# Layer norm weight and bias applied on ScalarE after the transpose, operand sums moved to VectorE, and other places for the turns

## What is computed

```
def _post(x, mix, ln1_g, ln1_b, w_up, w_down, ln2_g, ln2_b):
    h = _layernorm(DEEPNORM_ALPHA * x + mix, ln1_g, ln1_b)      # mix = concat(...) @ w_out
    f = square(relu(h @ w_up)) @ w_down
    return _layernorm(DEEPNORM_ALPHA * h + f, ln2_g, ln2_b)
```

## Time and profile before

| | us |
|---|---|
| median of 3 runs | 1950.86 (1946.68 to 1951.31) |
| profiled execution | 1942.62 |
| its span | 1940.8 |
| PE busy / DVE / ACT / POOL | 1752.3 / 1164.2 / 676.3 / 538.6 |
| mean granted TensorE clock | 0.948 |

### The profile page before, as it was taken

How to read it: one execution, slowest core, us unless ns; L and a number is a source line. 1 busy time by engine, 2 the same in 40 slices (tenths; PEclk the granted TensorE clock), 3 DMA queues, 4 the chain that set the end, 5 groups by cost and what they waited for, 6 DMA issues and landing times. The chain is left out here.

```text
span 1940.8 us, 41181 instructions
## 1 busy us (share of the span) xinstructions
PE 1752.3 (90%) x16969; PEld 1490.3 (77%) x16969; DVE 1164.2 (60%) x2079; ACT 676.3 (35%) x1467; POOL 538.6 (28%) x413
## 2 busy tenths in 40 slices
PE   6999996898899989988797996999999899989995
PEld 5999993676666666666576875999999888768884
DVE  7611025557776675665343898666666465565887
ACT  2221212344544544544232133322322244444441
POOL 0000003322232222222100455555565330322510
PEclk9999996898999999998698997999999999999997
DMA  5552230110111011010516231444444487555553
GB/s 189 187 192 95 73 95 20 49 49 14 70 63 61 2 61 62 2 61 13 149 24 240 91 116 44 131 138 144 150 126 125 146 287 237 166 176 164 194 183 121
DMA packets 155079, 218.86 MB, mean 113 GB/s; under 512 B 32290, under 2 KB 94394, under 8 KB 153876
## 3 DMA queue, kind: packets, MB, share of 16 engines
q1 hardware_dynamic: 153572, 211.53, 33.1%
q0 software_dynamic: 1328, 4.78, 0.6%
HBM read 151.66 MB, written 65.43 MB: 112 GB/s over the span
## 5 line engine op out<-in xcount | busy, mean ns | idle before, releaser
L1513 PE MATMUL c_p<-c_d_b_hi,c_d_a_hi 128*128 128x512 f32 x448 | 177.9, 397 | 14.2 <-DVE c_d_b_lo L1306 13.8
L1513 PE MATMUL c_p<-c_d_b_lo,c_d_a_hi 128*128 128x512 f32 x448 | 176.2, 393 | 0.0
L1513 PE MATMUL c_p<-c_d_b_hi,c_d_a_lo 128*128 128x512 f32 x448 | 175.9, 393 | 0.0
L1300 DVE TENSOR_TENSOR c_d_a_lo<-c_a_raw,c_d_a_hi 128x512 fp32r<-128x512 f32 x112 | 92.3, 824 | 62.4 <-ACT c_d_a_hi L1087 62.0
L1477 PE MATMUL c_p<-c_T_hi,c_up_op_hi 128*128 128x288 f32 x512 | 111.6, 300 | 12.7 <-DVE c_T_lo L1210 10.3
L1087 ACT ACTIVATE c_d_a_hi<-c_a_raw 128x512 fp32r<-128x512 f32 x112 | 70.2, 627 | 137.3 <-PE c_p L1513 128.2
L1513 PEld LDWEIGHTS c_p<-c_d_b_hi,c_d_a_hi 128*128 128x128 f32 x448 | 85.3, 190 | 37.1 <-issue 14.7
L1477 PE MATMUL c_p<-c_T_lo,c_up_op_hi 128*128 128x288 f32 x512 | 111.4, 300 | 0.0
L1477 PE MATMUL c_p<-c_T_hi,c_up_op_lo 128*128 128x288 f32 x512 | 111.3, 299 | 0.0
L1206 DVE TENSOR_TENSOR c_up_op_lo<-c_up_raw,c_up_op_hi 128x512 fp32r<-128x512 f32 x80 | 93.6, 1175 | 26.8 <-ACT c_up_op_hi L1022 26.8
L307 ACT ACTIVATE a_o<-a_pO 128x308 f32<-128x308 f32 (+1 forms) x80 | 32.7, 408 | 217.7 <-PE a_pO L446 200.9
(11 more groups left out here) (495 smaller groups left out, 4477.3 us busy)
## 6 DMA issues: line engine op xcount, KB each, us to landing
c_a_raw<-scratch_ops SPq DMA_DIRECT2D x112, 256.0 KB, 2.8
c_d_r<-w_down SPq DMA_DIRECT2D x96, 256.0 KB, 3.2
c_up_raw<-w_up SPq DMA_DIRECT2D x32, 512.0 KB, 5.2
scratch_ops<-c_hid SPq DMA_DIRECT2D x64, 256.0 KB, 2.5
scratch_ops<-c_h_sum SPq DMA_DIRECT2D x48, 256.0 KB, 2.0
scratch_p<-a_o SPq DMA_DIRECT2D x72, 154.0 KB, 1.8
m_pr<-w_in SPq DMA_DIRECT2D x8, 1232.0 KB, 7.8
m_pr<-scratch_p SPq DMA_DIRECT2D x8, 1232.0 KB, 5.3
```

What stands on the lines that cost most here:

```text
L1300: dve.tensor_tensor(lo[:, :], a_raw[a % 4][:, :], hi[:, :].bitcast(F32), ALU.subtract).then_inc(S("da_lo"), 1)
L1513: last = pe.matmul(bank, d_a[a % DA_RING][x][:, P * p:P * p + P], d_b[b % DB_RING][w][:, :], start=m in (1, 2, 5) and j == 0 and n == 0, s ...
```

## The change

- POOL's `h1` and DVE's `h1_last` go: all nine tiles end with DVE's normalise, are stored and turned without weight and bias. The store and the turn wait for `h1_normed`.
- ACT applies weight and bias in the turned layout, where they are one number per partition: `h1_copies` has one instruction per 128 columns with a scale and a bias pointer (columns of `ln1_g`, `ln1_b`, loaded as 128x8). The high parts for half 0 are then copied from SBUF.
- As the stored h1 lacks weight and bias, `prepare` on POOL applies them to the y tiles before `begin`: five tiles in round m = 1 behind the steps in `PREPARE_AT`, four behind the last step of round m = 6. The rows of `ln1_g` and `ln1_b` (512 KB each) are loaded behind step 4 of round m = 1 instead of in the output projection.
- `differences` and the T4 subtraction move from POOL to DVE; `w_sums(0)` also waits for the last `h1_normed`.
- `scales` for one column uses 9 small steps instead of 12.
- The turns move inside the out products, and turn 7 moves in; DVE's, ACT's and SP's orders follow. Products 4 and 5 are issued in halves.

In the diff the indentation is shortened.

```diff
@@ -491,6 +491,7 @@
+PREPARE_AT = (6, 8, 10, 12, 14)
@@ -501,8 +502,9 @@
 DA_RING, DB_RING, DR_RING = 4, 9, 8
-TURN_AT = {(3, 3): ("mix", 4), (4, 3): ("mix", 5), (4, 7): ("h1", 0), (5, 3): ("mix", 6), (5, 7): ("h1", 1), (6, 1): ("h1", 2),
-           (6, 3): ("mix", 7), (6, 5): ("h1", 3), (6, 7): ("h1", 4), (7, 3): ("mix", 8), (7, 7): ("h1", 5), (8, 3): ("h1", 6)}
+TURN_AT = {(3, 3): ("mix", 4), (4, 3): ("mix", 5), (4, 5): ("h1", 0), (4, 7): ("h1", 1), (5, 1): ("h1", 2), (5, 3): ("mix", 6),
+           (5, 6): ("h1", 3), (6, 1): ("h1", 4), (6, 3): ("mix", 7), (6, 6): ("h1", 5), (7, 3): ("mix", 8), (7, 6): ("h1", 6),
+           (8, 6): ("h1", 7)}
...
@@ -731,10 +734,7 @@
+    sp.wait_ge(S("h1_normed"), i + 1)
@@ -770,30 +770,31 @@
+    sp.dma_start(columns[n][:, :], io[n].rearrange("(k p) -> p k", p=P), allow_slow_non_contiguous=True).then_inc(S(f"{n}_landed"), 16)
 load_h(3)
...
@@ -878,6 +879,9 @@
         load_step(i, j)
+        if m == 1 and j == 4:
+            for n in ("ln1_g", "ln1_b"):
+                sp.dma_start(rows1[n][:, :], bcast(io[n])).then_inc(S(f"{n}_landed"), 16)
         if m == 1 and j == 5:
@@ -897,26 +901,16 @@
 -def h1(i):
-    if i == 0:
-        pool.wait_ge(S("ln1_g_landed"), 16)
-        pool.wait_ge(S("ln1_b_landed"), 16)
-    pool.wait_ge(S("h1_normed"), i + 1)
-    x = of(i)[:, :]
-    pool.tensor_tensor(x, x, rows1["ln1_g"][:, :], ALU.mult).then_inc(S("h1_scaled"), 1)
-    pool.wait_ge(S("h1_scaled"), i + 1)
-    pool.tensor_tensor(x, x, rows1["ln1_b"][:, :], ALU.add).then_inc(S("h1_ready"), 1)
...
+def prepare(n, T):
+    if n == 0:
+        pool.wait_ge(S("ln1_g_landed"), 32)
+        pool.wait_ge(S("ln1_b_landed"), 32)
+    pool.wait_ge(S(f"y_landed{T}"), 16)
+    x = y[T][:, :]
+    pool.tensor_tensor(x, x, rows1["ln1_g"][:, :], ALU.mult).then_inc(S("y_scaled"), 1)
+    pool.wait_ge(S("y_scaled"), n + 1)
+    pool.tensor_tensor(x, x, rows1["ln1_b"][:, :], ALU.add).then_inc(S("y_prepared"), 1)
@@ -924,6 +918,7 @@
         pool.wait_ge(S("out_summed"), N_TILE)
+        pool.wait_ge(S("h1_normed"), N_TILE)
     else:
@@ -951,14 +946,7 @@
-for i in range(7):
-    h1(i)
-for i in range(4, 8):
-    differences(i)
 w_sums(0)
-differences(8)
-pool.wait_ge(S("T2_summed"), 2)
-pool.tensor_tensor(HT["21"][:, :, :], HT["21"][:, :, :], HT["22"][:, :, :], ALU.subtract).then_inc(S("T4_summed"), 1)
 w_sums(1)
@@ -971,11 +959,16 @@
                 .then_inc(S("t_summed"), 1)
+            if j in PREPARE_AT:
+                prepare(PREPARE_AT.index(j), (SAMPLE_TILE, 0, 1, 2, 3)[PREPARE_AT.index(j)])
         if m == 6:
...
                 .then_inc(S("t_summed"), 1)
+            if j == NJ - 1:
+                for T in range(4, 8):
+                    prepare(T + 1, T)
         if m in (7, 4):
@@ -1002,12 +995,21 @@
+        if i == 0 and u == 0:
+            act.wait_ge(S("ln1_g_landed"), 16)
+            act.wait_ge(S("ln1_b_landed"), 16)
+        for k in range(KH):
+            c = slice(KH * u + k, KH * u + k + 1)
+            for half, src, cols in places(i):
+                last = act.activation(HT[quarter(u, half)][:, k, cols], bank[:, k, src], ACT.Identity,
+                                      scale=columns["ln1_g"][:, c], bias=columns["ln1_b"][:, c])
+        last.then_inc(S("h1_copied"), 1)
+    for u in range(2):
         for half, src, cols in places(i):
             if half == 0:
-                act.activation((B11, B21)[u][0][:, :, cols], bank[:, :, src], ACT.Copy).then_inc(S("side_hi"), 1)
-        for half, src, cols in places(i):
-            last = act.activation(HT[quarter(u, half)][:, :, cols], bank[:, :, src], ACT.Copy)
-        last.then_inc(S("h1_copied"), 1)
+                act.wait_ge(S("h1_copied"), copy_no["h1", i, u])
+                act.activation((B11, B21)[u][0][:, :, cols], HT[quarter(u, 0)][:, :, cols], ACT.Copy)\
+                   .then_inc(S("side_hi"), 1)
@@ -1048,28 +1050,27 @@
         h1_copies(t)
-    if (kind, t) == ("h1", 5):
+    if (kind, t) == ("h1", 6):
         act.wait_ge(S("out_summed"), 7)
         for q in range(3):
             up_high(q)
-act.wait_ge(S("out_summed"), 8)
-up_high(3)
-h1_copies(7)
+        act.wait_ge(S("out_summed"), 8)
+        up_high(3)
 act.wait_ge(S("out_summed"), N_TILE)
 act.wait_ge(S("h1_copied"), copy_no["h1", 7, 1])
 high(B22, HT["22"], EARLY_COLS, "B22_hi")
+h1_copies(8)
 act.wait_ge(S("T1_summed"), 4)
 high(T1, HT["11"], EARLY_COLS, "T1_hi")
+act.wait_ge(S("T2_summed"), 1)
+high(T2, HT["22"], EARLY_COLS, "T2_hi")
 up_high(4)
-h1_copies(8)
 act.wait_ge(S("h1_copied"), N_COPY)
 high(B22, HT["22"], LATE_COLS, "B22_hi")
-act.wait_ge(S("T2_summed"), 1)
-high(T2, HT["22"], EARLY_COLS, "T2_hi")
+act.wait_ge(S("T1_summed"), 5)
+high(T1, HT["11"], LATE_COLS, "T1_hi")
 act.wait_ge(S("T2_summed"), 2)
 high(T2, HT["22"], LATE_COLS, "T2_hi")
-act.wait_ge(S("T1_summed"), 5)
-high(T1, HT["11"], LATE_COLS, "T1_hi")
 up_high(5)
@@ -1176,8 +1177,16 @@
 def scales(t0, t1):
-    step(dve.tensor_scalar(mean[:, t0:t1, 1], mean[:, t0:t1, 1], LN_EPS, None, ALU.add))
-    rsqrt(dve, step, rstd[:, t0:t1], mean[:, t0:t1, 1], tmp[:, t0:t1])
+    v, r, t = mean[:, t0:t1, 1], rstd[:, t0:t1], tmp[:, t0:t1]
+    step(dve.tensor_scalar(v, v, LN_EPS, None, ALU.add))
+    if t1 > t0 + 1:
+        rsqrt(dve, step, r, v, t)
+        return
+    step(dve.tensor_scalar(half[:, :], v, -0.5, None, ALU.mult))
+    step(dve.tensor_scalar(r.bitcast(I32), v.bitcast(I32), -0.5, float(RSQRT_SEED), ALU.mult, ALU.add))
+    for _ in range(3):
+        step(dve.scalar_tensor_tensor(t, half[:, :], r, r, ALU.mult, ALU.mult))
+        step(dve.scalar_tensor_tensor(r, t, 1.5, r, ALU.add, ALU.mult))
@@ -1192,13 +1201,16 @@
-def h1_last(i):
...
+def differences(i):
+    cols = places(i)[-1][2]
+    dve.wait_ge(S("h1_copied"), copy_no["h1", i, 1])
+    dve.wait_ge(S("side_lo"), N_SIDE)
+    dve.tensor_tensor(HT["11"][:, :, cols], HT["12"][:, :, cols], HT["11"][:, :, cols], ALU.subtract)\
+       .then_inc(S("T1_summed"), 1)
+    dve.wait_ge(S("T1_summed"), i - 3)
+    dve.tensor_tensor(HT["12"][:, :, cols], HT["22"][:, :, cols], HT["12"][:, :, cols], ALU.subtract)\
+       .then_inc(S("T3_summed"), 1)
@@ -1257,41 +1269,48 @@
 h1(3)
+mix_low(6)
 side_low(0)
-mix_low(6)
+side_low(1)
 residual(4)
 h1(4)
-side_low(1)
 side_low(2)
-mix_low(7)
 residual(5)
 h1(5)
+mix_low(7)
 side_low(3)
 residual(6)
+h1(6)
+mix_low(8)
 side_low(4)
-mix_low(8)
-h1(6)
+differences(4)
+differences(5)
 residual(7)
-h1_last(7)
+h1(7)
 for q in range(4):
     up_low(q)
+differences(6)
 residual(8)
-h1_last(8)
-up_low(4)
+h1(8)
+differences(7)
 whole = slice(0, SIDE_T)
 low(B22, HT["22"], EARLY_COLS, "B22", 1)
 second_sum(EARLY_COLS, 1)
+up_low(4)
+low(T2, HT["22"], EARLY_COLS, "T2", 1)
+low(T1, HT["11"], EARLY_COLS, "T1", 1)
+differences(8)
 low(B22, HT["22"], LATE_COLS, "B22", 2)
 second_sum(LATE_COLS, 2)
-low(T2, HT["22"], EARLY_COLS, "T2", 1)
+low(T1, HT["11"], LATE_COLS, "T1", 2)
 low(T2, HT["22"], LATE_COLS, "T2", 2)
-low(T1, HT["11"], EARLY_COLS, "T1", 1)
-low(T1, HT["11"], LATE_COLS, "T1", 2)
 up_low(5)
 up_low(6)
 join(1)
+dve.wait_ge(S("T2_lo"), 2)
+dve.wait_ge(S("T2_summed"), 2)
+dve.tensor_tensor(HT["21"][:, :, :], HT["21"][:, :, :], HT["22"][:, :, :], ALU.subtract).then_inc(S("T4_summed"), 1)
 dve.wait_ge(S("T4_summed"), 1)
-dve.wait_ge(S("T2_lo"), 2)
 low(T3, HT["12"], whole, "T3", 1)
@@ -1322,7 +1341,7 @@
     x = half_of(T, n)
-    dve.wait_ge(S(f"y_landed{T}"), 16)
+    dve.wait_ge(S("y_prepared"), (T + 1) % N_TILE + 1)
     dve.scalar_tensor_tensor(x, x, ALPHA, bank, ALU.mult, ALU.add).then_inc(S("posted"), 1)
@@ -1409,10 +1428,7 @@
+            pe.wait_ge(S("h1_normed"), i + 1)
@@ -1446,7 +1462,7 @@
-def product(q):
+def product(q, hs=(0, 1)):
@@ -1465,7 +1481,7 @@
         elif m in (6, 5):
-            pe.wait_ge(S("T2_lo" if m == 6 else "T1_lo"), 2)
+            pe.wait_ge(S("T2_lo" if m == 6 else "T1_lo"), 1 if hs == (0,) else 2)
         elif m in (7, 4):
@@ -1473,11 +1489,12 @@
         for a, (w, x) in enumerate(((hi, B[m][0]), (hi, B[m][1]), (lo, B[m][0]))):
-            for h in range(2):
+            for h in hs:
                 last = pe.matmul(pS[U.slot[j, m]][:, h, 0:PIECE], w[:, k, :], x[:, k, PIECE * h:PIECE * h + PIECE],
                                  start=m in (1, 2, 5) and k == 0 and a == 0, stop=k == KH - 1 and a == 2,
                                  skip_group_check=True)
-    last.then_inc(S("u_done"), 1)
+    if 1 in hs:
+        last.then_inc(S("u_done"), 1)
@@ -1498,11 +1515,15 @@
     out_tile(i)
-turn("h1", 7)
-for q in range(3):
+for q in range(2):
     product(q)
 turn("h1", 8)
-for q in range(3, NQ - 2):
+for q in (2, 3):
+    product(q)
+for h in range(2):
+    product(4, (h,))
+    product(5, (h,))
+for q in range(6, NQ - 2):
     product(q)
```

41 lines of the change are left out of this document (9 added, 32 removed).

## The result

The changed kernel takes 1963.29 us, the median of 5 runs (1960.21 to 1970.92); the kernel before takes 1950.86 (1944.05 to 1952.32). The ratio is 1.0083, with a 95% interval of 1.0060 to 1.0105: slower by 0.8%. The forecast was 1967.4.

The account below looks back on a forecast made before the run. TensorE bounds the chain except where it stops, near the change for DVE, which two-input work shares exclusively with POOL. -6 + 17.4 + 5.1 = +16.5 on 1942.62 gives 1959.1, as a median 1967.4; 8 in 10: 1945 to 1978.

Parts of the forecast that it names:

- (1): Before the turns: weight and bias leave POOL, relieving DVE of 2.25 us per POOL instruction, mostly beside PE's slack.
- (2): ACT's scaling in the turned layout: 2.9 to 3.7 us a tile, about 5 for the sample tile; stalls 1.4 and 0.8.
- (3): PE's order and DVE's chain after the out products: tile 8 ends about 1152.1, product 4 moves from 1183.0 to 1177.5.
- (4): T4's subtraction moves from POOL to DVE: product 7 at about 1198.7 instead of 1203.46, 4.8 us earlier.
- 1.2 us for the clock: Behind product 7: a shorter stop saves part of PE's 7 us at clock 0.53, at most 3.3 us, 1.2 taken.
- Up stage: Sum of the gains up to product 7 and from the clock behind it: -6 us, between -3 and -10.
- (5): First down round, m = 1: five `prepare` on POOL hold DVE, and loads add delay; +17.4 us, between +11 and +20.
- (6): Round m = 5: four `prepare` behind the last sum of m = 6 hold DVE; +5.1 us, between +1.7 and +8.
- A: Rival: POOL's locks fit into DVE's idle time, the down rounds lose nothing, -6 us remains: 1944.9 us; chance 0.18.
- B: Rival: the first down round is only partly bound, half its loss, +8 us: 1958.8 us; chance 0.12.
- C: Rival: in-order waits eat the -6 us, or the weights' load starves steps 5 to 8; +25, 1976 us; chance 0.08.

Follow-up runs that it names:

- x6: Changed kernel with products 4 and 5 issued whole instead of by halves of the columns; 1963.67 us in a single execution, turn 159.7 us.
- x5: Changed kernel with `w_sums(0)` on POOL no longer waiting for the last `h1_normed`; 1964.11 us in a single execution, turn 158.0 us.
- x11: Changed kernel with weighting on DVE, T4's sum split and moved, and product 6's join ahead of T4's low part; median 1937.59 us, ratio 0.9949 to before.
- x1: Changed kernel without the `prepare` instructions and without the two loads of LN1's rows; median 1940.02 us, ratio 0.9962 to the kernel before.
- x3: Changed kernel without the two loads, with one POOL instruction per tile, reading y twice, instead of two; 1943.58 us.
- x10: Changed kernel with a third POOL instruction of 128x1024 behind the two of each `prepare`, adding the bias again; 1978.60 us.
- x4: Changed kernel with the residual's weighting on DVE in 36 instructions of 512 columns instead of on POOL, loads kept; median 1942.06 us, ratio 0.9952 to before.
- x2: Changed kernel without the two loads, its POOL instructions reading y twice instead of LN1's rows; 1949.71 us, round 1 115.5 us.
- x9: Changed kernel with weight and bias rows set to 1 and 0 by two POOL instructions instead of loaded; round 1 121.5 us.
- x7: Changed kernel without the `prepare` instructions but with the two loads of LN1's rows kept; 1943.13 us.

## Why the prediction was right, step by step

**(1), (2) The relief and ACT's scaling.** A tile takes 2.90 us and the sample tile 4.85 on ACT; forecast 2.9 to 3.7 and about 5. The two stalls on turns are 1.3 and 1.2 us; forecast 1.4 and 0.8.

**(3) The order of PE and the chain of DVE.** Product 4 starts at 1179.7; forecast 1177.5. DVE's chain began 1.7 us later than worked out (tile 8's products end at 1153.8, not 1152.1; 0.8 of it is the later start of the whole stage in this execution). The other 0.5 us lies within the chain and isn't traced further; POOL doesn't hold it at its end, since it is idle from 1168.5 to 1179.75. That product 4 waits for `copy_out(0)` is as worked out, and that the halves bring nothing is shown by x6.

**(4) Product 7** came at 1199.52, forecast 1198.7; from the first output product it moved by -4.7, forecast -4.8. The 1.2 us for the clock were too much: from product 7 to the first t1 sum 346.1 us stand against 346.5. Up stage -5.2 against -6. The 3.7 us that the prediction read in the earlier trace rows as a wait for a weight's low part end with a join as well: in before it starts at 1202.62, takes 0.74 us, and product 7 follows at 1203.46. x5 and x11 show that the order written here was not the best: 1.7 us lie in one wait, 6.0 in the places of T4's sums and of the join.

**(5) Round 1** is +18.8 us (16.4 to 18.9 over three executions), forecast +17.4. The spacing is 10.63 us, from the sum 2 x 3.12 + 2 x 2.25 = 10.74. Its mechanism is shown from five sides: no instruction, no loss (x1); one, hidden (x3); two, 2.5 us a pair over PE's 8.16; three, 4.6 us over (x10); and on DVE itself, nearly hidden (x4). The price per instruction of 1024 columns was close: (10.63 - 6.24) / 2 = 2.2 us, in x10 (12.8 - 6.24) / 3 = 2.2, in x2, whose instructions are half a us shorter, 1.7. That is each time the instruction's duration less 0.5 to 0.6 us. Term by term: from step 6 to step 15 the t1 sums take 49.95 us (1571.57 to 1621.52), forecast 50.6; PE's stop before step 15 is 6.15 us, forecast 6.7. The loads, taken at 0.7 (0 to 2.9) without a row for that share, cost 2.8 in the changed kernel's trace: this is the mis-sized term. The half clock after the stop is there (0.50 from 1620 to 1626). From step 15's sum to the first of m = 6 it is 48.4 us, where x3, which also waits for DVE at that place but at a clock of 1.00, needs 46.0: 2.4 us for the forecast 2.7, and 1.4 to 1.6 in x5, x6 and x9.

**(6) m = 5** is +3.0 us in this trace and +4.5 to +4.8 in x5, x6 and x9; forecast +5.1. DVE's last low part of m = 6 takes 2.17 us and ends 1.5 us later after POOL's last sum than in before, forecast 1.7. Two one-column steps were held, for 1.80 and 2.25 us; 2.3 each was worked out. x10 supports that the place is bound: four more instructions there add 7.4 us to it, 5.7 to 6.0 against x5, x6 and x9.

**Rivals.** A, the locks fit into idle time, decides at 1.9 us per `prepare`. x3, with about 1.4 (an instruction of 1.95 us less 0.6), shows it true below that point and x2, with 3.4, false above it. The Trainium skill (SBUF — State Buffer, section Who interferes with whom) calls the shared way to SBUF an exclusive lock, taken whole by whichever engine comes first; a DVE instruction with two inputs there contends with a POOL one that reads there. The rows of x5 and x10 agree, and so does the freedom of DVE's instructions with one SBUF input in x5. B and C are out by the stretches: the loss in round 1 is that of the full sum. The median alone would not tell, since 1963.29 lies about halfway between B's 1958.8 and the forecast.

**Luck in the sum.** Measured by stretches the change is +16.8 us where +16.5 was forecast. The single terms are not that close: up stage -5.2 for -6, round 1 +18.8 for +17.4, m = 5 +3.0 for +5.1. Their errors cancel, and in x5, x6 and x9 the last two come out otherwise (16 to 19, and about 4.6).

**The level.** From the profiled execution the forecast was 1959.1, and the changed kernel's profiled execution took 1960.21. The 4.1 us by which 1967.4 lies over the median 1963.29 come from the last step: the 8.2 us between before's profiled execution and its median were added whole, and for the changed kernel that difference is 3.1. What an execution lies under the median is not a property of the kernel; x4's profiled execution lay 7.3 us over its own. Nor is a median of five sharp to a few us: beside the experiments the kernel before ran 17 to 23 times each on three chips, with medians of 1947.9 to 1948.8.

## What to carry to other kernels

Before work is moved to GpSimd "because it is idle", take a step that is bound by TensorE, write down what VectorE and GpSimd together need in it where VectorE reads two SBUF tiles, and add the moved instruction's time to that sum: below the step's length it is free (x3), above it most of each us counts (2.2 of 2.7 us for the third instruction of x10). If the sum exceeds, look for VectorE itself in short pieces before giving up the change; here that turned +0.8% into -0.2 to -0.5%. And look at each wait of GpSimd for what VectorE is doing when it ends: four weight sums beside statistics and PSUM reads held VectorE for 1.3 us (x5), and the same work 6 us later for 2.9.

## What the runs showed of the hardware that was not expected

- A GpSimd instruction of 128x1024 with one tile as both inputs takes 1.89 to 2.35 us in x2 and x3, with two different tiles 2.35 to 2.91 us in the changed kernel.
- A transfer of 1 MB delays VectorE by about 3 us in x7 and costs nothing, and costs 0.5 to 3.0 us where VectorE has no time left: its price depends on what else was added.
- At a granted clock of 1.00 the same up products run at two speeds. Busy time by stretch, of x7 and then of the changed kernel:

```profile
1300.00:1400.00 100.00, 100.00 (x771) 100.00 (x771) 75.15 (x66) 30.61 (x51) 64.63 (x40) 1.00 0.42 130
...
1288.00:1388.00 100.00, 100.00 (x752) 100.00 (x751) 65.70 (x64) 29.94 (x50) 58.56 (x37) 1.00 0.42 129
```

x7 does 771 matmuls in 100 us, the changed kernel 752, with the same code in this stage; its long run of 2472 matmuls took 323.2 us against 331.3 (331.3 in x1 too). At the first t1 sum 6.9 us of that are left, and they are the 7 us by which x7's "rest" lies under x1's. No run here shows the cause; it is a spread larger than the 0.3% that an edit was to be told by, and single executions are read by stretches here for that reason.
